# Moving two thirds of the ada sums of a 256-token network into its first feed-forward part, with two-part fp32r row sums

## The chip, the cores and the metric

The kernel runs on one core of a Trainium2 chip. The metric is the device time of one execution in microseconds. TensorE does the matrix products, VectorE and ScalarE the elementwise work, POOL (GpSimd) issues some transfers and does a few elementwise steps, SP (SyncE) issues the transfers of the weights. Each engine runs its own instructions in order and waits on semaphores.

## The reference

One sequence of 256 tokens of width 1024 passes a first block of two layers and a second block of one layer. Everything is fp32. What matters here:

```
# first block, layer 0: even mixer; layer 1: odd mixer (two attentions)
x = layer_norm(ALPHA * x + mixer(x), ln_mix_g[l], ln_mix_b[l])
x = layer_norm(ALPHA * x + (silu(x @ w_gate[l]) * (x @ w_up[l])) @ w_down[l], ln_ffn_g[l], ln_ffn_b[l])

# second block
mod = split(silu(c) @ ada_w + ada_b, 6)                  # six rows of 1024
a = rmsnorm(x, g_pre) * (1 + mod[1]) + mod[0]
x = x + mod[2] * rmsnorm(short_gated_conv(a), g_post)
f = (relu(modulate(rmsnorm(x, g_pre_ff), mod[3], mod[4]) @ mlp_w_in) ** 2) @ mlp_w_out
x = x + mod[5] * rmsnorm(f, g_post_ff)
```

`silu(c) @ ada_w` is a vector of 1024 times a matrix of 1024 x 6144 (24 MB).

## The kernel before, in words

The program is one sequence of stages: even mixer, first feed-forward part (`ffn0`), odd mixer, second feed-forward part (`ffn1`), short conv (`sc`), MLP. Weights come in chunks of 1 MB. SP loads a chunk (`raw`) as soon as a slot of its ring of four or six is free. ScalarE copies it to fp32r (`hi`), VectorE subtracts (`lo = raw - hi`); this is a *split*. TensorE then does three fp32r products for one fp32 product (hi·hi, hi·lo, lo·hi). `split(upto)` stands at written-out places in the programs of ScalarE and VectorE, so the order is that of the code: no scheduler is involved, and an instruction that waits holds back all behind it on its engine.

A feed-forward part has 11 blocks (`NF`), one per 256 columns of the hidden layer. In block `i` TensorE does the gate chunk and the up chunk (`col`, 48 matmuls of 256 columns each) into PSUM banks 6 and 7 or 4 and 5 in turn; ScalarE does silu, VectorE the product `hid`, ScalarE `hid_hi`, VectorE `hid_lo`. Up to block 8 TensorE then does the down chunk of the block before (`rows_full`, 24 matmuls of 512 columns). Blocks 9 and 10 have none; after block 10 the last three down chunks are done for token half 0 and then for half 1, the third one closing each half (`rows_end`). The layer norm's sum (`ln_sum`, L1645) reads that.

The ada product is done beside `ffn1`: POOL loads 24 pieces of ada_w, 1 MB each, in turn into the buffers `sq` and `r`; VectorE multiplies each by a column of silu(c) and adds it into `modrow` (`ada_step`, L423), two or three per block. `mod_sums(m)` (L699) sums row m over the 128 partitions with a matmul against ones, into the PSUM banks that the block before has just left, and `mod_copy` (L1217) on ScalarE brings the sum, now on all partitions, back to `modrow`. The table `MOD_AT = {4: 0, 5: 1, 7: 2, 8: 3, 10: 4}` says after which block which row is summed; the sixth is in `sc`. TensorE does not write the banks again before the copy. At the end of `ffn1` VectorE does `gained` (L1723) for rows 1 and 2: it multiplies them by two gain rows, which POOL loads into `sq` after the last ada product (`gain_row`, L482). Behind `gained` VectorE has the split of the last down chunk, two more splits and then `ln_sum`.

POOL also loads the two rows (gain and bias) of each layer norm into `lnrow` (`ln_rows`, L478), those of the next norm as soon as the one before is through.

`modrow` lies in memory that the even and the odd mixer use for other things; it is free only in the feed-forward parts and behind them.

Of the kernel before, what the change touches and what calls it, by code (L numbers as in the profile page):

```python
# [6 lines left out]
F32 = mybir.dt.float32  # L7
# [62 lines left out]
def build(nc, A, out):  # L70
    ctx = ExitStack()
    with ctx:
# [24 lines left out]
        ones = sb("ones", [P, P])  # L97
        d_skip = sb("d_skip_sb", [P, KT])
# [99 lines left out]
        def bank2(b):  # L198
            return PS[:, b, :].rearrange("p (a s) -> p a s", a=2)

# [212 lines left out]
        ADA_BLOCKS = range(1, 10)  # L413
        MOD_AT = {4: 0, 5: 1, 7: 2, 8: 3, 10: 4}
        MOD_LAST = 5
# [57 lines left out]
        def _(pool):  # L473
# [46 lines left out]

            pool.wait_ge(*sig_at("ln0", "x", 4))
            ln_rows("ln1")
            pool.wait_ge(*sig_at("ln1", "x", 4))
# [5 lines left out]
            pool.tensor_tensor(kr_cos[rr, :], kr[rr, 0, :], cos, ALU.mult).then_inc(sem("kr_cos"), 1)  # L529
            pool.wait_ge(*norm("kvn", "var", 1))  # L530
            for q in range(4):
# [3 lines left out]
                    .then_inc(sem("qm_cos"), 1)  # L535
# [3 lines left out]
                             .to_broadcast([32, MLA_H, S])).then_inc(sem("kr_rot"), 1)  # L539

            pool.wait_ge(*sig_at("ln2", "x", 4))
            ln_rows("ln3")
            pool.memset(modrow[:, :, :], 0.0).then_inc(sem("ada_zero"), 1)
            pool.wait_ge(sem("ada_zero"), 1)
            pool.dma_start(modrow[0:1, :, :].rearrange("p m d -> p (m d)"), A["ada_b_2"][0:1, :])\
                .then_inc(sem("ada_bias"), 16)
            for n in range(ADA_N):
                if n >= 2:
                    pool.wait_ge(sem("ada_fma"), n - 1)
                pool.dma_start(ada_raw[n % 2], A["ada_w_2"][0][n % KT * P:(n % KT + 1) * P, n // KT * CH:(n // KT + 1) * CH])\  # L550
                    .then_inc(sem(f"ada_landed{n % 2}"), 16)
# [8 lines left out]
        def _(pe):  # L560
# [134 lines left out]
            def mod_sums(m, bank):  # L695

                pe.wait_ge(sem("ada_fma"), KT * (m // 2 + 1))
                for n in range(2):
                    last = pe.matmul(PS[:, bank + n, :], ones[:, :], modrow[:, m, n * HB:(n + 1) * HB], start=True, stop=True)  # L699
                last.then_inc(sem("mod_sum"), 1)  # L700

            def ffn(name, operand, after, src):
# [13 lines left out]
                for i in range(1, NF):  # L716
                    b = 6 - 2 * (i % 2)
                    pe.wait_ge(hid_done, o + i)
                    if name == "ffn1" and i - 1 in MOD_AT:
                        pe.wait_ge(sem("mod_row"), MOD_AT[i - 1] + 1)  # L720
# [5 lines left out]
                    if name == "ffn1" and i in MOD_AT:  # L726
                        pe.wait_ge(hid_done, o + i + 1)
                        mod_sums(MOD_AT[i], 6 - 2 * ((i - 1) % 2))
# [164 lines left out]
            base = first["odd"]  # L893
            for h in range(2):
# [83 lines left out]
            def scores(a):  # L978
# [5 lines left out]
                if a == FOX_H:  # L984
                    pe.wait_ge(sem("odd_evac"), 19)
                    pe.wait_ge(sem("kr_rot"), 1)
# [54 lines left out]
            ffn("ffn1", "ln2", "pre", r_tok)  # L1041

# [20 lines left out]
            for q in range(1, 4):  # L1063
                for part in range(3):
                    col(at["sc", "c", q] + part, sc_bank(3 * q + part), x_hi, x_lo)
                    if q == 1 and part == 0:
# [4 lines left out]
                        mod_sums(MOD_LAST, 0)  # L1071
                if q == 1:
                    pe.wait_ge(sem("mod_row"), MOD_LAST + 1)
# [45 lines left out]
        def _(act):  # L1119
# [19 lines left out]
            def preload(func):  # L1139

                act.wait_ge(sem("eps_set"), 1)
# [71 lines left out]

            def mod_copy(m, bank):
# [5 lines left out]
            def ffn(name):  # L1220
# [11 lines left out]
                for i in range(1, NF):  # L1232
                    g = at[name, "g", i]
                    split(g + 2)
                    act.wait_ge(chunk_used, g + 1)
# [8 lines left out]
                    if name == "ffn1" and i in MOD_AT:  # L1244
                        mod_copy(MOD_AT[i], 6 - 2 * ((i - 1) % 2))
# [17 lines left out]
            act.activation(head_vec[:, 2:3], head_vec[:, 1:2], ACT.Exp).then_inc(sem("a_ready"), 1)  # L1263
# [8 lines left out]
            act.activation(silu_c[:, :], vecs[:, 2, 0:8], ACT.Silu).then_inc(sem("silu_c_ready"), 1)  # L1272
# [868 lines left out]
```

## Time and profile before

| | us |
|---|---|
| median of 3 runs | 980.95 |
| lowest, highest | 979.12, 981.13 |
| profiled execution | 980.15 |
| its span, first to last instruction | 978.27 |
| TensorE matmul busy in the span | 944.3 (97%) |
| VectorE busy | 645.9 (66%) |
| ScalarE busy | 466.6 (48%) |
| mean granted TensorE clock | 0.997 |

Times inside the span count from its first instruction. "Busy" of TensorE counts matmuls that overlap one another; the distance from one start to the next is what a matmul costs in a row of them. `idle before` in a timeline names what ended the idle time of the engine. A row of a timeline may merge several instructions (xN). `ffn0` lies at about 150 to 330 us, `ffn1` at about 495 to 690, `sc` at 690 to 790.

### The profile page before, as it was taken

What the parts mean: (1) busy time and instruction counts of PE and PEld (TensorE: products, weight loads), DVE (VectorE), ACT (ScalarE), POOL (GpSimd) and SP (SyncE); (2) the same over time, 40 slices, a digit from 0 to 9 for tenths busy, and PEclk for the clock granted to TensorE, in tenths of its full rate; (3) what the DMA queues carried; (4) which work ended last, traced back from release to release, by engine and by line L of the source; (5) the groups of instructions that cost most, each with busy time, mean ns of one, the idle gap of its engine ahead of it and who ended that gap; (6) DMA issues with size and microseconds to landing.
All of it is one profiled execution on the core that took longest, in us unless ns stands there. A gap on an engine that the chain in (4) does not pass through costs nothing.

```text
span 978.3 us, 15123 instructions
## 1 busy us (share of the span) xinstructions
PE 944.3 (97%) x6537; PEld 862.8 (88%) x6537; DVE 645.9 (66%) x737; ACT 466.6 (48%) x577; POOL 62.0 (6%) x79
## 2 busy tenths in 40 slices
PE   6999989999999999999899999999899999999997
PEld 6999879999999799876699989998799989999986
DVE  4976896645454863676659788788866865555554
ACT  6556744434343465755544343445344644444442
POOL 2034000000000000220030001000000000000000
PEclk9999999999999999999999999999999999999999
DMA  9744466565565453412579999995566456566531
GB/s 280 239 131 130 136 205 219 186 195 178 181 203 177 130 173 110 133 44 87 176 283 331 381 317 338 308 348 165 185 198 198 130 175 213 175 194 191 174 128 44
DMA packets 122282, 190.52 MB, mean 195 GB/s; under 512 B 6566, under 2 KB 103080, under 8 KB 119144
## 3 DMA queue, kind: packets, MB, share of 16 engines
q1 hardware_dynamic: 115184, 156.94, 49.5%
q0 software_dynamic: 5616, 31.78, 8.8%
q8 instruction: 52, 0.85, 0.3%
q10 hardware_dynamic: 1416, 0.83, 0.3%
q14 instruction: 14, 0.11, 0.0%
HBM read 188.49 MB, written 1.05 MB: 194 GB/s over the span
## 4 chain that ended last, share of the span: by engine, by line
PE 80%; DVE 10%; ACT 5%; issue 3%; DMA 1%; DVEq 0%; POOL 0%; ACTq 0%
PE PS L565 15%; PE PS L567 15%; PE PS L566 15%; PE PS L572 10%; PE PS L574 9%; PE PS L573 9%; DVE lo L1575 3%; ACT hi L1136 2%; PE PS L699 1%; PE PS L663 1%; DMA raw<-even_w_in 1%; DVE r L1645 1%; ACT hid L1437 1%; DMA sq<-norm_gains 1%; ACT sq L1321 1%
## 5 line engine op out<-in xcount | busy, mean ns | idle before, releaser
L1575 DVE TENSOR_TENSOR lo<-raw,hi 128x2048 fp32r<-128x2048 f32 (+2 forms) x150 | 336.1, 2258 | 168.8 <-ACT hi L1136 168.6
L565 PE MATMUL PS<-x_hi,hi 128*128 128x256 f32 x1320 | 374.4, 284 | 1.9 <-DVE x_lo L1772 1.9
L567 PE MATMUL PS<-x_hi,lo 128*128 128x256 f32 x1320 | 372.3, 282 | 0.0
L566 PE MATMUL PS<-x_lo,hi 128*128 128x256 f32 x1320 | 371.7, 282 | 0.0
L1136 ACT ACTIVATE hi<-raw 128x2048 fp32r<-128x2048 f32 (+2 forms) x150 | 278.1, 1880 | 10.2 <-DMA raw<-even_w_in 8.0
L565 PEld LDWEIGHTS PS<-x_hi,hi 128*128 128x128 f32 x1320 | 251.2, 190 | 4.3 <-DVE lo L1575 2.3
L566 PEld LDWEIGHTS PS<-x_lo,hi 128*128 128x128 f32 x1320 | 251.2, 190 | 1.9 <-issue 0.5
L567 PEld LDWEIGHTS PS<-x_hi,lo 128*128 128x128 f32 x1320 | 251.2, 190 | 0.0
L572 PE MATMUL PS<-hi,hid_hi 128*128 128x512 f32 x352 | 141.2, 401 | 1.1 <-DVE lo L1575 0.7
L574 PE MATMUL PS<-hi,hid_lo 128*128 128x512 f32 x352 | 138.6, 394 | 0.0
L573 PE MATMUL PS<-lo,hid_hi 128*128 128x512 f32 x352 | 138.5, 393 | 0.0
L572 PE MATMUL PS<-hi,x_hi 128*128 128x256 f32 (+1 forms) x256 | 81.7, 319 | 7.7 <-DVE x_lo L1674 3.5
L572 PEld LDWEIGHTS PS<-hi,hid_hi 128*128 128x128 f32 x352 | 66.1, 188 | 17.5 <-issue 3.7
L574 PEld LDWEIGHTS PS<-hi,hid_lo 128*128 128x128 f32 x352 | 66.0, 188 | 15.6
L574 PE MATMUL PS<-hi,x_lo 128*128 128x256 f32 (+1 forms) x256 | 79.8, 312 | 0.0
L573 PE MATMUL PS<-lo,x_hi 128*128 128x256 f32 (+1 forms) x256 | 79.6, 311 | 0.0
L573 PEld LDWEIGHTS PS<-lo,hid_hi 128*128 128x128 f32 x352 | 66.0, 188 | 15.1 <-issue 1.2
L1238 ACT ACTIVATE gate_s<-PS 128x512 f32<-128x512 f32 x20 | 12.0, 599 | 103.2 <-PE PS L567 103.2
L572 PEld LDWEIGHTS PS<-hi,x_hi 128*128 128x128 f32 x256 | 48.8, 191 | 13.3 <-issue 8.1
L574 PEld LDWEIGHTS PS<-hi,x_lo 128*128 128x128 f32 x256 | 48.8, 191 | 2.8
L1243 ACT ACTIVATE hid_hi<-hid 128x512 fp32r<-128x512 f32 x20 | 12.6, 632 | 80.9 <-DVE hid L1750 80.9
L573 PEld LDWEIGHTS PS<-lo,x_hi 128*128 128x128 f32 x256 | 49.0, 191 | 2.5
(280 smaller groups left out, 825.5 us busy)
## 6 DMA issues: line engine op xcount, KB each, us to landing
raw<-ffn_w_gate SPq DMA_DIRECT2D x22, 1024.0 KB, 5.4
raw<-ffn_w_up SPq DMA_DIRECT2D x22, 1024.0 KB, 5.5
raw<-ffn_w_down SPq DMA_DIRECT2D x22, 1024.0 KB, 5.0
raw<-mlp_w_in SPq DMA_DIRECT2D x16, 1024.0 KB, 5.6
raw<-mlp_w_out SPq DMA_DIRECT2D x16, 1024.0 KB, 5.0
sq<-ada_w POOLq DMA_DIRECT2D x12, 1024.0 KB, 6.3
r<-ada_w POOLq DMA_DIRECT2D x12, 1024.0 KB, 7.2
raw<-sc_w_in SPq DMA_DIRECT2D x12, 1024.0 KB, 5.3
```

The source lines that it names most:

```text
L565: pe.matmul(dst, wh, hi, start=start, stop=False, skip_group_check=True)
L566: pe.matmul(dst, wh, lo, start=False, stop=False, skip_group_check=True)
L567: return pe.matmul(dst, wl, hi, start=False, stop=stop_, skip_group_check=True)
L572: pe.matmul(dst, hi, wh, start=start, stop=False, skip_group_check=True)
L573: pe.matmul(dst, hi, wl, start=False, stop=False, skip_group_check=True)
L574: return pe.matmul(dst, lo, wh, start=False, stop=stop_, skip_group_check=True)
L663: last = pe.transpose(PS[:, 2 * h + n, j * P:(j + 1) * P], src[:, h, o:o + P], ident)
L699: last = pe.matmul(PS[:, bank + n, :], ones[:, :], modrow[:, m, n * HB:(n + 1) * HB], start=True, stop=True)
L1136: act.activation(split_view("hi", c), split_view("raw", c), ACT.Copy).then_inc(hi_split, 1)
L1238: act.activation(gate_s[:, i % 2, :, :], bank2(6 - 2 * (i % 2)), ACT.Silu).then_inc(silu, 1)
L1243: act.activation(hid_hi[:, i % 3, :, :], hid[:, i % 2, :, :], ACT.Copy).then_inc(hi_done, 1)
L1575: dve.tensor_tensor(split_view("lo", c), split_view("raw", c), split_view("hi", c).bitcast(F32), ALU.subtract)\
```

## The change

- The 24 ada products are divided: 16 (rows 0 to 3) run beside `ffn0`, two in each of blocks 1 to 8, and 8 (rows 4 and 5) beside `ffn1`, one in each of blocks 1 to 8. POOL clears `modrow` and loads the bias row in two parts.
- `MOD_AT` now has a table for each part: in `ffn0` rows 0 to 3 after blocks 6, 7, 9, 10; in `ffn1` rows 4 and 5 after blocks 9 and 10. The sum in `sc` is gone.
- Before a sum, ScalarE rounds the row to fp32r (`mod_high`) and VectorE takes the remainder (`mod_low`) into `mod_part`; `mod_sums` is four fp32r matmuls against `ones_r`.
- `mod_part` shares its memory with `lnrow`. So `ln_rows("ln1")` waits for the fourth sum and `ln_rows("ln3")` for the sixth, where each used to be issued before the part began.
- Rows 0 to 3 are written to a DRAM tensor `mods` after `ffn0` and read back, onto all partitions, at the start of `ffn1`. VectorE and ScalarE wait for the write before they use that memory in the odd stage.
- Some semaphores are merged (`cleared`, `rope_cos`, `a_silu_c`), with the same order of what is waited for.

```diff
-        lnrow = sb("lnrow", [P, 2, D])
+        with ExitStack() as row_views:
+            lnrow = sb("lnrow", [P, 2, D], F32, row_views)
+        mod_part = sb("mod_part", [P, 2, D], F32R)
...
+        mods = nc.dram_tensor("mods", (1, 4 * D), F32, kind="Internal").ap()
...
-        ADA_BLOCKS = range(1, 10)
-        MOD_AT = {4: 0, 5: 1, 7: 2, 8: 3, 10: 4}
-        MOD_LAST = 5
+        ADA_STEPS = {"ffn0": (0, 2 * KT), "ffn1": (2 * KT, ADA_N)}
+        MOD_AT = {"ffn0": {6: 0, 7: 1, 9: 2, 10: 3}, "ffn1": {9: 4, 10: 5}}
...
+            def ada_loads(m0, m1):
+                pool.memset(modrow[:, m0:m1, :], 0.0).then_inc(sem("ada_zero"), 1)
+                pool.wait_ge(sem("ada_zero"), 1 + (m0 > 0))
+                pool.dma_start(modrow[0:1, m0:m1, :].rearrange("p m d -> p (m d)"), A["ada_b_2"][0:1, m0 * D:m1 * D])\
+                    .then_inc(sem("ada_bias"), 16)
+                if m0:
+                    pool.wait_ge(sem("mods_moved"), 16)
+                    pool.dma_start(modrow[:, 0:4, :].rearrange("p m d -> p (m d)"), mods[0:1, :].to_broadcast([P, 4 * D]))\
+                        .then_inc(sem("mods_moved"), 16)
+                for n in range(m0 * KT // 2, m1 * KT // 2):
...
             pool.wait_ge(*sig_at("ln0", "x", 4))
+            ada_loads(0, 4)
+            pool.wait_ge(sem("mod_sum"), 4)
             ln_rows("ln1")
+            pool.wait_ge(sem("mod_row"), 4)
+            pool.dma_start(mods[0:1, :], modrow[0:1, 0:4, :].rearrange("p m d -> p (m d)")).then_inc(sem("mods_moved"), 16)
             pool.wait_ge(*sig_at("ln1", "x", 4))
             ln_rows("ln2")
...
             pool.wait_ge(*sig_at("ln2", "x", 4))
+            ada_loads(4, 6)
+            pool.wait_ge(sem("mod_sum"), 6)
             ln_rows("ln3")
...
             def mod_sums(m, bank):
-                pe.wait_ge(sem("ada_fma"), KT * (m // 2 + 1))
+                pe.wait_ge(sem("mod_low"), m + 1)
                 for n in range(2):
-                    last = pe.matmul(PS[:, bank + n, :], ones[:, :], modrow[:, m, n * HB:(n + 1) * HB], start=True, stop=True)
+                    for part in range(2):
+                        last = pe.matmul(PS[:, bank + n, :], ones_r[:, :], mod_part[:, part, n * HB:(n + 1) * HB],
+                                         start=part == 0, stop=part == 1, skip_group_check=True)
...
+            def mod_high(m):
+                act.wait_ge(sem("ada_fma"), KT * (m // 2 + 1))
+                if m:
+                    act.wait_ge(sem("mod_sum"), m)
+                act.activation(mod_part[:, 0, :], modrow[:, m, :], ACT.Copy).then_inc(sem("mod_high"), 1)
...
+            def mod_low(m):
+                dve.wait_ge(sem("mod_high"), m + 1)
+                dve.tensor_tensor(mod_part[:, 1, :], modrow[:, m, :], mod_part[:, 0, :].bitcast(F32), ALU.subtract)\
+                   .then_inc(sem("mod_low"), 1)
...
+            dve.wait_ge(sem("mods_moved"), 16)
             dve.memset(neg_both[:, :].bitcast(F32), 0.0)
```

POOL's program at the end of `ffn1`, before the change (`sq<-norm_gains` are the gain rows that `gained` needs, `lnrow<-norm_gains` two later ones):

```order
L550 DMA sq<-ada_w 128x2048 [waits ada_fma]
L550 DMA r<-ada_w 128x2048 [waits ada_fma]
L482 DMA sq<-norm_gains 128x1024 [waits ada_fma]
L482 DMA sq<-norm_gains 128x1024
L482 DMA lnrow<-norm_gains 128x1024 [waits ln_x]
```

And after it:

```order
L538 DMA sq<-ada_w 128x2048 [waits ada_fma]
L538 DMA r<-ada_w 128x2048 [waits ada_fma]
L482 DMA lnrow<-ln_ffn_g 128x1024 [waits mod_sum]
L482 DMA lnrow<-ln_ffn_b 128x1024
L486 DMA sq<-norm_gains 128x1024 [waits ada_fma]
L486 DMA sq<-norm_gains 128x1024
L486 DMA lnrow<-norm_gains 128x1024 [waits ln_x]
```

ln3's two rows have moved from the head of `ffn1` to a place ahead of the gain rows, behind a wait for the sixth sum.

VectorE's program at the same end, after the change (L1788 is `hid`, L1754 `gained`, L1603 a split, L1673 `ln_sum`); apart from the line `mod_part` its order there is that of before:

```order
L1760 TENSOR_TENSOR mod_part<-modrow,mod_part 128x1024 [waits mod_high]
L1603 TENSOR_TENSOR lo<-raw,hi 128x2048 [waits hi_split]
L1788 TENSOR_TENSOR hid<-gate_s,PS 128x512 [waits chunk_used,ffn_silu]
L1793 TENSOR_TENSOR hid_lo<-hid,hid_hi 128x512 [waits ffn_hid_hi]
L1754 SCALAR_TENSOR_TENSOR modrow<-modrow,sq 128x1024 [waits gain_landed,mods_moved] x2
L1603 TENSOR_TENSOR lo<-raw,hi 128x2048 [waits hi_split] x3
L1673 SCALAR_TENSOR_TENSOR r<-x_tok,PS 128x512 [waits ffn1_acc,gained]
```

TensorE's program from block 9 to block 10 of `ffn0`, before:

```order
L565 MATMUL PS<-x_hi,hi 128x256
L566 MATMUL PS<-x_lo,hi 128x256
L567 MATMUL PS<-x_hi,lo 128x256
L565 MATMUL PS<-x_hi,hi 128x256 [waits lo_split,ffn_hid]
L566 MATMUL PS<-x_lo,hi 128x256
```

And after:

```order
L582 MATMUL PS<-x_hi,hi 128x256
L583 MATMUL PS<-x_lo,hi 128x256
L584 MATMUL PS<-x_hi,lo 128x256
L717 MATMUL PS<-mod_part,ones_r 128x512 [waits mod_low,ffn_hid]
L717 MATMUL PS<-mod_part,ones_r 128x512 x3
L582 MATMUL PS<-x_hi,hi 128x256 [waits lo_split,mod_row,ffn_hid]
L583 MATMUL PS<-x_lo,hi 128x256
```

A sum stands directly between the two blocks, and the next block's first matmul waits for `mod_row`, ScalarE's copy of it.

## Rows read from the trace of the kernel before

**Rows 1.** The page, busy time and share of the span by engine.
```profile
PE 944.3 (97%) x6537; PEld 862.8 (88%) x6537; DVE 645.9 (66%) x737; ACT 466.6 (48%) x577; POOL 62.0 (6%) x79
```

**Rows 2.** Chain of waits: start us, us, what.
```profile
665.65 5.46 DMA sq<-norm_gains
...
717.84 1.72 PE PS L699 x4
```

**Rows 3.** Timeline of TensorE, last block of `ffn1`: start us, us, instruction.
```profile
668.07 1.88 PE L699 MATMUL PS<-modrow,ones 128*128 128x512 f32 x4
...
670.02 0.40 PE L573 MATMUL PS<-lo,hid_hi 128*128 128x512 f32 x1
670.25 0.39 PE L574 MATMUL PS<-hi,hid_lo 128*128 128x512 f32 x1
```

**Rows 4.** Timeline of VectorE, end of `ffn1`.
```profile
668.34 0.69 DVE L1750 TENSOR_TENSOR hid<-gate_s,PS 128x512 f32<-128x512 f32 x1 [1.10 <-PE PS L567]
...
671.21 2.36 DVE L1723 SCALAR_TENSOR_TENSOR modrow<-modrow,sq 128x1024 f32<-128x1024 f32 x2 [0.79 <-DMA sq<-norm_gains]
673.49 6.69 DVE L1575 TENSOR_TENSOR lo<-raw,hi 128x2048 fp32r<-128x2048 f32 x3
680.09 1.28 DVE L1645 SCALAR_TENSOR_TENSOR r<-x_tok,PS 128x512 f32<-128x512 f32 x2
...
688.71 1.28 DVE L1645 SCALAR_TENSOR_TENSOR r<-x_tok,PS 128x512 f32<-128x512 f32 x2
```

**Rows 5.** Timeline of TensorE, the three last down chunks of `ffn1`.
```profile
675.91 0.47 PE L572 MATMUL PS<-hi,hid_hi 128*128 128x512 f32 x1 [0.37 <-DVE lo L1575]
...
686.89 0.39 PE L574 MATMUL PS<-hi,hid_lo 128*128 128x512 f32 x1
```

**Rows 6.** Timeline of ScalarE, end of `ffn1`.
```profile
669.06 0.63 ACT L1243 ACTIVATE hid_hi<-hid 128x512 fp32r<-128x512 f32 x1 [4.15 <-DVE hid L1750]
669.98 1.03 ACT L1217 ACTIVATE modrow<-PS 128x1024 f32<-128x1024 f32 x1 [0.29 <-PE PS L699]
```

**Rows 7.** Timeline of ScalarE in `ffn0`: first ordinary block, last block.
```profile
167.22 0.59 ACT L1238 ACTIVATE gate_s<-PS 128x512 f32<-128x512 f32 x1
...
312.19 0.60 ACT L1238 ACTIVATE gate_s<-PS 128x512 f32<-128x512 f32 x1 [2.53 <-PE PS L567]
...
318.74 0.63 ACT L1243 ACTIVATE hid_hi<-hid 128x512 fp32r<-128x512 f32 x1 [4.15 <-DVE hid L1750]
319.28 5.51 ACT L1136 ACTIVATE hi<-raw 128x2048 fp32r<-128x2048 f32 x3
```

**Rows 8.** Timeline of ScalarE in `ffn1`: first ordinary block, last block.
```profile
510.48 0.59 ACT L1238 ACTIVATE gate_s<-PS 128x512 f32<-128x512 f32 x1
...
662.51 0.60 ACT L1238 ACTIVATE gate_s<-PS 128x512 f32<-128x512 f32 x1 [2.53 <-PE PS L567]
```

**Rows 9.** Timeline of POOL: clearing of modrow, first ada load, gain rows.
```profile
495.57 5.24 POOL L543 MEMSET modrow<- 128x6144 f32 x1
...
501.60 0.56 POOL L550 DMA_DIRECT2D sq<-ada_w  x1
...
665.13 1.05 POOL L482 DMA_DIRECT2D sq<-norm_gains  x2 [12.58 <-DVE modrow L423]
```

**Rows 10.** Timeline of VectorE, end of `ffn0`: first use of ln1's row.
```profile
330.58 1.41 DVE L1658 SCALAR_TENSOR_TENSOR r<-r,moments,lnrow 128x512 f32<-128x512 f32 x2
```

**Rows 11.** DMA issues from 480 to 520 us: count, size, us to landing.
```profile
r<-ada_w POOLq DMA_DIRECT2D x1, 1024.0 KB, 10.0
lnrow<-ln_ffn_g POOLq DMA_DIRECT2D x1, 512.0 KB, 4.0
lnrow<-ln_ffn_b POOLq DMA_DIRECT2D x1, 512.0 KB, 4.9
```

**Rows 12.** Busy by stretch; last: granted clock, DMA share, GB/s.
```profile
666.00:673.00 7.00, 7.00 (x37) 5.45 (x36) 4.42 (x5) 3.65 (x4) 0.18 (x1) 1.00 1.03 344
```

**Rows 13.** The same for a stretch before `ffn0`; first column TensorE busy (matmuls).
```profile
133.50:136.90 3.40, 3.40 (x10) 2.63 (x9) 3.30 (x4) 0.00 (x0) 0.00 (x0) 0.50 0.00 0
```

More of the change, by code:

```diff
@@ L725, in ffn @@
                     col(at[name, "g", i] + 1, b + 1, x_hi, x_lo)
-                    if name == "ffn1" and i in MOD_AT:
+                    if i in MOD_AT[name]:
                         pe.wait_ge(hid_done, o + i + 1)
-                        mod_sums(MOD_AT[i], 6 - 2 * ((i - 1) % 2))
+                        mod_sums(MOD_AT[name][i], 6 - 2 * ((i - 1) % 2))
                     if i <= NF - TAIL:
@@ L1234, in ffn @@
                     split(g + 2)
+                    if i in MOD_AT[name]:
+                        mod_high(MOD_AT[name][i])
                     act.wait_ge(chunk_used, g + 1)
@@ L1261, in _ @@
             act.wait_ge(sem("heads_landed"), 16 * 3)
-            act.activation(head_vec[:, 2:3], head_vec[:, 1:2], ACT.Exp).then_inc(sem("a_ready"), 1)
+            act.activation(head_vec[:, 2:3], head_vec[:, 1:2], ACT.Exp).then_inc(sem("a_silu_c"), 1)
             split(3)
@@ L1271, in _ @@
             act.wait_ge(sem("vecs_ready"), 1)
-            act.activation(silu_c[:, :], vecs[:, 2, 0:8], ACT.Silu).then_inc(sem("silu_c_ready"), 1)
+            act.activation(silu_c[:, :], vecs[:, 2, 0:8], ACT.Silu).then_inc(sem("a_silu_c"), 1)
             base = first["even"]
@@ L1719, in gained @@
             def gained(m, i, plus):
-                dve.wait_ge(sem("mod_row"), m + 1)
+                if m < 4:
+                    dve.wait_ge(sem("mods_moved"), 32)
+                else:
+                    dve.wait_ge(sem("mod_row"), m + 1)
                 dve.wait_ge(sem("gain_landed"), 32 * (i // 2 + 1))
@@ L1731, in ffn @@
                     g = at[name, "g", i]
-                    ada = list(range(ADA_N * (i - 1) // 9, ADA_N * i // 9)) if name == "ffn1" and i in ADA_BLOCKS else []
-                    if ada and i == 1:
-                        dve.wait_ge(sem("silu_c_ready"), 1)
-                        dve.wait_ge(sem("ada_bias"), 16)
+                    n0, n1 = ADA_STEPS[name]
+                    ada = list(range(n0 + (n1 - n0) * (i - 1) // 8, n0 + (n1 - n0) * i // 8)) if 1 <= i <= 8 else []
+                    if i == 1:
+                        dve.wait_ge(sem("a_silu_c"), 2)
+                        dve.wait_ge(sem("ada_bias"), 16 + 16 * (name == "ffn1"))
                     split(g + 2)
-                    if len(ada) > 2:
-                        ada_step(dve, ada.pop(0))
                     if i == 0:
@@ L1746, in ffn @@
                     else:
+                        if i in MOD_AT[name]:
+                            mod_low(MOD_AT[name][i])
                         split(g + 3)
```

63 lines of the change are left out of this document (30 added, 33 removed).

## The prediction, made before the result was known

> **What bounds the kernel now.** I read the page's busy times first: TensorE is busy for 97% of the span and VectorE for 66% [rows 1]. So a matmul removed in the middle of a stage counts in full, and VectorE or a DMA counts only where TensorE waits for it. The chain of waits says where that is: one such place is the end of the second feed-forward part. There the chain leaves TensorE and runs over the transfer of two gain rows, 5.46 us, and later passes the fp32 row sum in the short-conv stage, 1.72 us [rows 2]. The timelines of each engine at that end (about 668 us) then give the order and the spare time.
>
> I call T the start of the row sum in the last block, 668.07 us [rows 3]. From there: VectorE starts `hid` at T+0.27, scales the two modulation rows by the gains (`gained`) at T+3.14, splits three weight chunks from T+5.42 and starts the layer norm's sum at T+12.02 [rows 4]. The first of the three chunks is the last one that TensorE needs: it resumes at 675.91 (T+7.84), after a last wait of 0.37 us [rows 5]. So the end is VectorE's, and whatever delays `gained` delays both. The profiled run took 980.15 us, of which the span is 978.27; it lies 0.8 below the median of the runs, 980.95. The sum is made against 980.15.
>
> **The change, part by part.**
>
> *The sums.* Before, one `mod_sums` is two fp32 matmuls, in the profile four records 0.43 us apart, 1.72 us. After, it is four fp32r matmuls of 128x512. Such matmuls start 0.23 us apart [rows 3], so 0.93 us.
> - Second part: four sums at blocks 4, 5, 7, 8 go, 4 x 1.72 = -6.88. The fifth sits after T, in time that VectorE covers.
> - Short-conv stage: the sixth goes, -1.72 [rows 2]. The next chunk's split is then ready only about 0.1 us after TensorE could use it, so I take -1.6.
> - First part: rows 0 and 1 at blocks 6 and 7 are followed by 5.6 us of down-projection, which hides the copy back: 2 x 0.93 = +1.86.
> - Rows 2 (first part) and 4 (second part) are put in block 9. After block 9 no down-projection comes, and the next block's first matmul writes the very PSUM banks of the sum, behind a wait for ScalarE's copy out of them. That copy stands behind `hid_hi`. In the last block `hid_hi` starts at T+0.99 and lasts 0.63, and the copy lasts 1.03 [rows 6]. The same order at block 9 ends the copy 0.99+0.63+1.03 = 2.65 us after the block's matmuls, in place of 0. So 2 x 2.65 = +5.30, of which 3.4 is TensorE standing still. Before, no sum stood in block 9.
> - Row 3, first part's last block: the copy now stands between `hid_hi` (318.74) and the three splits behind it (319.28) [rows 7]. VectorE waits for those splits, so +0.95 (1.03 less the overlap of neighbouring instructions).
>
> Subtotal: -6.88 - 1.6 + 1.86 + 5.30 + 0.95 = -0.37 us. The cheaper sums are eaten by where they stand.
>
> *The 16 products moved, with 16 MB of loads.* The second part already carried 24 in nine blocks: its first ordinary block's gate to its last took 662.51-510.48 = 152.03 us, less 6.88 of sums 145.15, against 312.19-167.22 = 144.97 in the first part without any [rows 7, 8]. So this load costs 0.2 us at most, and taking it off gives 0.2 at most: 0. `mod_high` and `mod_low`, one pass over 128x1024 each on ScalarE and VectorE (1.03 us for the copy of that size [rows 6]), lie in the same idle time. The clearing of modrow took 5.24 us for 6144 columns [rows 9], so 3.5 for 4096; with the bias it ends about 160, before the second block needs it: 0.
>
> *Rows through DRAM.* The write goes out after the first part's last copy, and the waits for it (VectorE before its memsets, ScalarE before v_tok; behind them all the odd stage's splits) come behind the layer norm that ends the part; that of the second part starts its sum at T+12.02 [rows 4]. Even the slowest landing below, 10 us, is hidden: 0, bounded by 0 and 0.5. The read back is 2 MB ahead of the ada loads; the ln3 rows that stood there (1 MB) are gone and the clearing is 3.5 us shorter, so the first product still finds its data: 0, up to +2.
>
> *ln1's rows* are now requested after the fourth sum, about T+1.4. In the first part's clock their use is at 330.58 [rows 10], 12.8 us after its T (318.74 less the 0.99 above, 317.75). They need 4.9 us alone [rows 11], 10 with competition: hidden.
>
> *ln3's rows and the gain rows.* This is the largest term. POOL is in order. Before, it issued the two gain rows at 665.13 [rows 9], T-2.94, straight after the last product. After, it first waits for the sixth sum, which ends T+0.93 plus 0.2, then issues ln3's two rows, then the two gain rows. With POOL's reaction of 0.3 the first issue is T+1.41 and the first gain row T+2.47: 5.41 us later than before. Behind `gained` on VectorE stand the last down chunk's split, which TensorE waits for, two more splits and the layer norm's sum.
> Lower bound of the shift S of `gained`: 5.41, if the landing takes what it took. Upper: 2 MB of rows share the engines with the 1 MB weight chunk that SP issues around T. The engines moved 344 GB/s while the gain rows and that chunk ran [rows 12]; a rate of 300 to 330 for 3.15 MB beginning at T+2 gives T+11.5 to T+12.5, and with landing and start T+13.4: S = 10.3. The nearest row: two 1 MB ada loads beside SP's chunks, the first issued at 501.60 and the second half a microsecond later [rows 9], of which the second landed 10.0 us after its issue, so 10.6 after the first [rows 11]. The same 2 MB in the same company: T+1.41+10.6 = T+12.0. I take S = 8.7, between that and the rate. TensorE then stands still for some 9 us.
>
> On this the Trainium skill has two sayings in "DMA: Bandwidth & Descriptors". "Issuing engines are not separate DMA queues": POOL's rows and SP's chunk run on the same 16 engines and interleave; the trace agrees, with its 10.0 against 4.9 us, and that speaks against the change. "Anatomy of one DMA — SWDGE (gpsimd) path" fits 2.0 us plus bytes over 436 GB/s: for the four rows together an estimate of 6.8 us, thus S of about 5; the sum would be 985 instead of 988.5.
>
> **Sum:** 980.15 - 0.37 + 8.7 = 988.5 us.
>
> **The rivals.**
> 1. *Quick rows.* The four rows overlap so well that the gain rows land as they did: S = 5.4. For it: one pair lands in 4.0 and 4.9 us [rows 11]. Against it: that was 1 MB alone. 980.15-0.37+5.4 = 985.2.
> 2. *The clock falls.* After sparse matmuls the granted clock was 0.50 from 133.5 to 136.9, 10 matmuls in 3.4 us where 14.6 fit [rows 13]. The new stop of 9 us at the second part's end could do the same. TensorE's last tail matmul starts at 686.89 [rows 5], 1.8 us before VectorE's second half (688.71) [rows 4], so 1.5 us lost is hidden; with the low clock for twice as long, 1.1 shows: 989.6. The Trainium skill ("TensorE: Matmul & The Clock Gate", "HAM oscillation — how this bites in real kernels") says that long DMA waits put the gate back to half speed; in this trace only that one stretch inside the work shows it.
> 3. *Crowding at the second part's start.* The 2 MB read back takes 6.1 us at 344 GB/s [rows 12] and pushes chunks or the first product out by that; if their lead covers half of it, +2 to +3: 991. Against it: the 1 MB of ln3's rows that stood there before is gone.
> 4. *Faster: the gain rows land before VectorE asks.* `gained` would start at T+2.3 behind `hid_lo`, S = -0.8: 979.0. It decides at S = 0.37, where the rows cost what the sums give. Against it: they would have to land in 2.1 us after the first issue, and the fastest landing is 4.0 [rows 11]. Relief of VectorE in the second part would be the only other gain, and that is 0.2 at most.
> 5. *The change does less than it says*, that is, the rows were never waited for at either end and all else cancels: 980. For it only that the subtotal is near zero.
>
> **How the numbers follow.** Forecast 0.60, quick rows 0.17, clock 0.05, crowding 0.09, faster 0.05, nothing 0.04. A measurement of this kernel can tell about 0.2% (2 us) from no change. The forecast and rivals 1 to 3 are slower by more than that: 0.91; faster 0.05; within 0.04. The forecast's own range, S from 7 to 10.3, is 986.8 to 990.1. The range asked for reaches down to the quick rows less half a microsecond and up to crowding: 984.5 to 991.5.
>
> **What would show it.** The sums' four matmuls 0.23 us apart. A gap of about 1.7 us on TensorE ahead of the last gate chunk in both parts, released by ScalarE's modrow copy. At the end of the second part: POOL issuing four rows after the last sum, VectorE idle 8 to 9 us before L1754 (`gained`), released by DMA sq<-norm_gains, and TensorE idle about 9 us before the last down chunk. In the first part no idle time before L1686 released by a lnrow transfer. No wait of POOL, ACT or VectorE named by mods longer than 0.5 us. The prediction is wrong if the two parts' VectorE load turns out to hold up TensorE, if `gained` starts within 6 us of T, or if block 9 shows no gap.

## The result and the profile after

The changed kernel takes 992.73 us, the median of 4 runs (991.3 to 993.05), against 980.95 for the kernel before: ratio 1.0118, 95% interval 1.0104 to 1.0133. I had forecast 988.5 and a range up to 991.5. The direction was right, the size 4.2 us short, and the time lies outside the range. Beside the experiments the kernel before was run again, 15, 17 and 23 times; the medians are 981.28, 981.35 and 981.36 (979.25 to 983.4 in all).

The profiled run of the changed kernel took 992.73 us, so the two traces differ by 12.58. TensorE's busy time has not grown, only its share [rows 1]:

```profile
PE 944.8 (95%) x6537; PEld 866.6 (87%) x6537; DVE 652.2 (66%) x744; ACT 471.7 (48%) x583; POOL 62.3 (6%) x83
```

**The end of the second feed-forward part.** The chain of waits, start, length and what, answers to the first row of [rows 2]. Where 5.46 us of transfer stood, there are now 9.97, and ahead of them POOL's issues, released by the sum (L717):

```profile
671.02 0.95 PE PS L717 x4
671.97 0.28 issue
672.25 1.05 POOL lnrow L482 x2
673.30 0.51 POOL sq L486
673.81 9.97 DMA sq<-norm_gains
```

T, the start of the sum in the last block, is 670.86 here. VectorE's timeline in the same place, against [rows 4]:

```profile
671.13 0.69 DVE L1788 TENSOR_TENSOR hid<-gate_s,PS 128x512 f32<-128x512 f32 x1 [1.11 <-PE PS L584]
...
683.88 2.36 DVE L1754 SCALAR_TENSOR_TENSOR modrow<-modrow,sq 128x1024 f32<-128x1024 f32 x2 [10.67 <-DMA sq<-norm_gains]
686.15 6.69 DVE L1603 TENSOR_TENSOR lo<-raw,hi 128x2048 fp32r<-128x2048 f32 x3
```

`gained` (L1754) starts at T+13.02 in place of T+3.14: a shift of 9.88 us, where I had 8.7. TensorE stands still for 11 us, and when it resumes its matmuls take longer than the 0.39 us of [rows 5]:

```profile
688.59 0.77 PE L589 MATMUL PS<-hi,hid_hi 128*128 128x512 f32 x1 [11.06 <-DVE lo L1603]
689.15 0.63 PE L590 MATMUL PS<-lo,hid_hi 128*128 128x512 f32 x1
689.58 0.63 PE L591 MATMUL PS<-hi,hid_lo 128*128 128x512 f32 x1
```

The stretches show why; the columns are stretch, length, busy time of PE, PEld, VectorE, ScalarE and POOL, then the granted clock, DMA share and GB/s:

```profile
676.00:688.00 12.00, 1.53 (x7) 0.92 (x5) 4.12 (x3) 4.27 (x4) 0.00 (x0) 0.71 0.47 162
688.00:694.00 6.00, 5.42 (x13) 4.29 (x14) 5.44 (x4) 0.00 (x0) 0.00 (x0) 0.50 0.01 3
694.00:696.00 2.00, 2.00 (x9) 1.58 (x8) 1.88 (x4) 0.00 (x0) 0.00 (x0) 0.82 0.00 0
```

The granted clock fell during the stop, at 681.0, and stayed at 0.50, the lower of the two levels, for the first 6.1 us of the tail (688.59 to 694.7): a matmul every 0.43 us in place of 0.23. That is the second rival, and it came on top of the forecast. Part of what it cost can be seen on VectorE. In the kernel before, the two instructions of the layer norm's sum follow each other with no wait [rows 4]; here the second one waits 0.64 us for TensorE's last matmul of the half:

```profile
692.76 0.68 DVE L1673 SCALAR_TENSOR_TENSOR r<-x_tok,PS 128x512 f32<-128x512 f32 x1
694.08 0.69 DVE L1673 SCALAR_TENSOR_TENSOR r<-x_tok,PS 128x512 f32<-128x512 f32 x1 [0.64 <-PE PS L591]
```

**Block 9.** TensorE's timeline: the sum, and then the next gate chunk's first matmul.

```profile
656.64 1.09 PE L717 MATMUL PS<-mod_part,ones_r 128*128 128x512 f32 x4
659.27 0.36 PE L582 MATMUL PS<-x_hi,hi 128*128 128x256 f32 x1 [1.53 <-issue]
```

From the sum's start it is 2.63 us, where I had 2.65; the gap itself is 1.53 us, where I had 1.7. The wait is put down to "issue"; ScalarE's timeline shows what ended it, the copy out of the banks behind `hid_hi`, in the order of [rows 6]:

```profile
657.63 0.63 ACT L1271 ACTIVATE hid_hi<-hid 128x512 fp32r<-128x512 f32 x1 [4.04 <-DVE hid L1788]
658.16 1.00 ACT L1243 ACTIVATE modrow<-PS 128x1024 f32<-128x1024 f32 x1
```

**The whole, stage by stage.** I compared the start of each block's `gate_s` in both traces. The difference grows by 1.50 up to the first part (153.28 to 154.78), then by 0.92, 0.92, 2.71 and, by the start of the second part, 0.92. In the second part it falls by four times 1.71 or 1.72 and grows by 2.70 at block 9. From that part's last block to short-conv it grows by 11.18, and in short-conv it falls by 1.36. Sum: 12.6.

The first 1.50 arise where both kernels have the same code, 1.3 of them between 12 and 18 us. In the trace before, TensorE does 10 matmuls a microsecond from 12 us on; in the other it does 6 or 7 until 15 us. The first line is of the trace before, the second of the trace after:

```profile
12.00:13.00 1.00, 1.00 (x10) 1.00 (x10) 1.00 (x3) 1.00 (x3) 0.00 (x0) 1.00 1.10 370
12.00:13.00 1.00, 1.00 (x7) 1.00 (x6) 1.00 (x3) 1.00 (x3) 0.00 (x0) 1.00 1.09 369
```

The 1.00 of the granted clock is no reading here: its record begins at 10.6 us in the trace before and only at 15.4 in the other. Fewer matmuls up to just that moment fit a lower clock before it; no experiment tested this.

### The profile page after: what moved, and what is told of

Its sections match the earlier page's. It is cut to its first block, busy times and chain, and to the rows that moved or that the text cites. A ratio compares the mean times of both kernels' runs of the same rounds, so it can differ in the third digit from the quotient of the medians.

```text
span 990.8 us, 15148 instructions
## 1 busy us (share of the span) xinstructions
PE 944.8 (95%) x6537; PEld 866.6 (87%) x6537; DVE 652.2 (66%) x744; ACT 471.7 (48%) x583; POOL 62.3 (6%) x83
## 4 chain that ended last, share of the span: by engine, by line
PE 82%; DVE 8%; ACT 5%; issue 3%; DMA 2%; POOL 0%; DVEq 0%; ACTq 0%
PE PS L582 16%; PE PS L584 16%; PE PS L583 16%; PE PS L589 10%; PE PS L590 10%; PE PS L591 10%; DVE lo L1603 2%; ACT hi L1155 2%; DMA sq<-norm_gains 1%; PE PS L680 1%; DMA raw<-even_w_in 1%; ACT hid L1465 1%; ACT sq L1349 1%; DVE gate_s L2024 1%; PE PS L1040 0%
## 5 line engine op out<-in xcount | busy, mean ns | idle before, releaser
L1603 DVE TENSOR_TENSOR lo<-raw,hi 128x2048 fp32r<-128x2048 f32 (+2 forms) x150 | 336.1, 2258 | 169.9 <-ACT hi L1155 169.7
L590 PEld LDWEIGHTS PS<-lo,hid_hi 128*128 128x128 f32 x352 | 66.7, 190 | 14.3
```

The source lines that it names most:

```text
L590: pe.matmul(dst, hi, wl, start=False, stop=False, skip_group_check=True)
L1603: dve.tensor_tensor(split_view("lo", c), split_view("raw", c), split_view("hi", c).bitcast(F32), ALU.subtract)\
```

## The experiments

Runs differ by up to 3.3 us before the first feed-forward part begins: its first `gate_s` starts at 152.90 to 156.15 us in the thirteen profiles, in no relation to the edits. Six profiles start by 153.68, and in them the record at 1.00 begins at 9.7 to 10.6 us; seven start at 154.68 or later, and in them it begins, or comes back from 0.50, only at 15.2 to 17.5 us. So the table gives, beside the medians, the profiled run's time less that start, which is free of it. It is not free of low clock later on: in the profiles of gain_early and filler a stretch at 0.50 inside the odd stage (422.7 to 426.1, 425.2 to 428.6) adds 1.0 us that the others do not have. Each ratio is the recorded one, against the runs of the kernel before of the same round (for `after` the 4 of the first); it is not the quotient of the two medians.

```
kernel            median   ratio to before (95%)      profiled less start
before            981.36   (last 23 runs)              826.87
after             992.73   1.0118 (1.0104, 1.0133)    837.95
gain_early        980.60   0.9995 (0.9985, 1.0006)    826.87
gain_first_late   988.59   1.0077 (1.0058, 1.0096)    833.24
off_nine          987.65   1.0070 (1.0055, 1.0086)    834.06
filler            994.84   1.0145 (1.0126, 1.0164)    841.73
filler95          992.41   1.0108 (1.0090, 1.0126)    837.74
chunk_later       990.40   1.0090 (1.0073, 1.0106)    835.25
fp32_sums         983.66   1.0018 (1.0008, 1.0028)    829.02
both              977.30   0.9957 (0.9942, 0.9972)    822.38
gained_last       982.99   1.0018 (1.0008, 1.0029)    828.30
late_copy         976.38   0.9964 (0.9950, 0.9978)    821.40
all_second        980.75   0.9997 (0.9983, 1.0011)    827.72
```

**gain_early: the gain rows at their old place**

```
             ada_loads(4, 6)
+            pool.wait_ge(sem("ada_fma"), ADA_N)
+            gain_row(0)
+            gain_row(1)
             pool.wait_ge(sem("mod_sum"), 6)
             ln_rows("ln3")
-            pool.wait_ge(sem("ada_fma"), ADA_N)
-            gain_row(0)
-            gain_row(1)
```

> The changed kernel, with POOL's two gain rows issued right behind the last ada product, ahead of its wait for the sixth sum; ln3's two rows stay behind that wait. Account A (the 11.2 us lost at the end of the second feed-forward part are VectorE's wait for the gain rows, 9.9 us, and 1.3 us of low clock after TensorE's stop): gained starts near T+3.1 again, no low clock at that end, 992.7 - 11.2 = 981.5 us. Rival B (ln3's rows, still late, are needed by the layer norm and take the gain rows' place): VectorE idle before L1686 for 3 us or more, 984.5 or above. Rival C (the wait is for the traffic as a whole, not for the order on POOL): gained still 5 us late, 987.

980.60 us: the two moved lines take back 12 us. VectorE's timeline at that end:

```profile
671.67 0.69 DVE L1793 TENSOR_TENSOR hid_lo<-hid,hid_hi 128x512 fp32r<-128x512 f32 x1 [0.70 <-ACT hid_hi L1271]
672.28 2.35 DVE L1754 SCALAR_TENSOR_TENSOR modrow<-modrow,sq 128x1024 f32<-128x1024 f32 x2
```

`gained` follows `hid_lo` with no wait, at T+2.27 (T is 670.01): 0.87 earlier than in the kernel before, where it waited 0.79 for the rows. The stage is 0.9 us shorter than in the kernel before, where in the changed kernel it was 11.2 longer. ln3's rows, still issued after the sum, are nowhere waited for, which ends rival B; rival C falls too. The clock is 1.00 through the tail; it goes to 0.50 from 692.3 to 695.7, at the start of short-conv, where no lost time is seen.

**gain_first_late: the gain rows ahead of ln3's, both late**

```
             pool.wait_ge(sem("mod_sum"), 6)
-            ln_rows("ln3")
             pool.wait_ge(sem("ada_fma"), ADA_N)
             gain_row(0)
             gain_row(1)
+            ln_rows("ln3")
```

> The changed kernel, with the wait for the sixth sum kept ahead of all four rows, but the two gain rows issued before ln3's two. Splits the late issue from the traffic ahead. If the rows stand in line on one queue and move at 268 GB/s behind SP's chunk (as in the trace of the changed kernel), the gain rows land near T+8.7, shift of gained 5.6 instead of 9.9, 992.7 - 4.3 = 988.4 us, or 987.1 if TensorE's clock then holds. If the queue order doesn't matter (all four share): no change, 992.5. If one pair lands in 4.9 us whatever SP does: shift 3.3, 986 or 985.

988.59 us. The order on the queue counts: `gained` starts at T+9.69, a shift of 6.55, one us more than expected. POOL's queue still stands in line; no pair of rows came in 4.9 us. TensorE's first tail matmul was at 683.53, and the clock:

```profile
676.00:684.00 8.00, 0.47 (x1) 0.50 (x2) 5.17 (x4) 2.56 (x3) 0.00 (x0) 0.72 0.50 203
684.00:686.00 2.00, 2.00 (x6) 1.52 (x6) 2.00 (x2) 0.00 (x0) 0.00 (x0) 0.50 0.00 0
686.00:688.00 2.00, 2.00 (x10) 1.60 (x9) 2.00 (x2) 0.00 (x0) 0.00 (x0) 0.89 0.03 8
```

The clock fell here too, but was back 2.9 us after the first tail matmul. The stage takes 6.53 us longer than before, the shift and nothing more, and VectorE does not wait for TensorE in the layer norm's sum:

```profile
687.71 1.28 DVE L1673 SCALAR_TENSOR_TENSOR r<-x_tok,PS 128x512 f32<-128x512 f32 x2
```

**off_nine: rows 2 and 4 summed at block 8**

```
-        MOD_AT = {"ffn0": {6: 0, 7: 1, 9: 2, 10: 3}, "ffn1": {9: 4, 10: 5}}
+        MOD_AT = {"ffn0": {6: 0, 7: 1, 8: 2, 10: 3}, "ffn1": {8: 4, 10: 5}}
...
-  n0 + (n1 - n0) * (i - 1) // 8, n0 + (n1 - n0) * i // 8)) if 1 <= i <= 8
+  n0 + (n1 - n0) * (i - 1) // 7, n0 + (n1 - n0) * i // 7)) if 1 <= i <= 7
```

> The changed kernel, with rows 2 and 4 summed at block 8 in place of block 9 and the products spread over seven blocks instead of eight (up to three in a block). Account A (at block 9 TensorE stands still for the copy, 2.71 us a place; at block 8 a down-projection covers it, 0.92): 992.7 - 2 x 1.79 = 989.1 us. Rival: the three products in a block, or the scaling to two parts, hold up VectorE and through it TensorE at block 8: 991 to 993.

987.65 us, and 3.9 less than the changed kernel by the profiles, for 3.6 expected. In the first part 0.92 comes at block 8 and 2.71 goes at block 9; in the second 0.87 comes and 2.77 goes. That block 9 costs a stop and block 8 none is shown; three products in a block hold nothing up here.

**filler and filler95: TensorE kept at work during the stop**

Matmuls of constants into a bank that is free there; their result isn't used.

```
+                        if name == "ffn1" and not h:
+                            for n in range(150):      # filler95: 95
+                                pe.matmul(PS[:, 6, 0:P], ones_r[:, :], ones_r[:, :], start=True, stop=True)
                         rows_end(*down(i), h, name)
```

> The changed kernel, with 150 matmuls of 128x128 of constants on TensorE ahead of the last down chunk of the second feed-forward part, where it stands idle for 11 us; their result is not used. Account A (1.3 us of the loss are the low clock, 0.50 until 694.3, after the stop): the granted clock stays 1.00 to the end of the tail and the time falls by about 1.3 to 991.4 us. Rival (those 1.3 us are hidden behind VectorE's layer norm, or are something else): 992.7, with the clock at 1.00.

> As the filler before, with 95 matmuls of 128x128 in place of 150: in the profile of that run one took 0.111 us, so 95 take 10.5 us and end before the 11.2 us of waiting do. Account A (low clock costs 1.3 us): granted clock 1.00 through the tail, the end of the second feed-forward part loses 9.9 us in place of 11.2, 992.7 - 1.3 = 991.4 us. Rival (the slow tail is hidden behind VectorE): 992.7.

The first was a miss of mine: one such matmul takes 0.111 us, so 150 ran until 695.7 and held up the tail itself, 994.84 us. It shows one thing: with no gap the granted clock stayed at 1.00 through the stop and the tail.

```profile
680.00:690.00 10.00, 10.00 (x92) 10.00 (x91) 2.80 (x3) 1.90 (x3) 0.00 (x0) 1.00 0.39 153
688.00:694.00 6.00, 6.00 (x56) 6.00 (x56) 6.00 (x5) 0.00 (x0) 0.00 (x0) 1.00 0.00 0
```

With 95 the matmuls ended at 688.49, and as the rows landed a microsecond later in that run (`gained` at T+14.04, shift 10.90), TensorE stood idle for 1.41 us. Of the filler95 profile:

```profile
688.00:690.00 2.00, 0.59 (x6) 0.45 (x5) 2.00 (x2) 0.00 (x0) 0.00 (x0) 0.84 0.00 0
690.00:692.00 2.00, 2.00 (x5) 1.61 (x6) 2.00 (x2) 0.00 (x0) 0.00 (x0) 0.50 0.00 0
692.00:694.00 2.00, 2.00 (x8) 1.60 (x8) 2.00 (x2) 0.00 (x0) 0.00 (x0) 0.80 0.00 0
```

The clock fell after all, but came back 2.9 us into the tail, and the stage took 10.89 us longer for a shift of 10.90: nothing on top. The median of 992.41 tells no difference from 992.73, since the later landing ate the gain. So the expectation failed as to the clock and the time; what holds is a comparison over the profiles. Where the low clock lasts 2.9 us of the tail (gain_first_late, filler95) the stage loses the shift and no more, and VectorE does not wait for TensorE there; where it lasts 6.1, 5.9 and 5.5 us (the changed kernel, off_nine, chunk_later) the stage loses 1.3, 1.2 and 1.0 us more than the shift, and in all three VectorE has the wait of 0.64 us. No run took the low clock away and left the late rows as they were, so the 1.3 us rest on this comparison.

**chunk_later: SP's weight chunk held back**

```
+                if c == first["sc"] + 2:
+                    sp.wait_ge(sem("gain_landed"), 32)
```

In the changed kernel POOL issued the rows from 672.25 on. The queues of the DMA engines (queue, packets, MB, share), first from 671 to 675, then from 676 to 684:

```profile
q1 hardware_dynamic: 858, 0.88, 71.0%
...
q0 software_dynamic: 540, 1.95, 70.7%
```

Until 675 only SP's chunk moves (q1), though POOL had issued all four rows by 674.3; from 676 on only POOL's rows, 1.95 MB in some 8 us. In the microsecond between, both move:

```profile
q1 hardware_dynamic: 182, 0.17, 50.0%
q0 software_dynamic: 36, 0.15, 40.4%
```

Their first packet starts at 675.21, 2.96 us after the first issue.

> The changed kernel, with SP's third short-conv chunk (1 MB, issued at T+0.2) held until the two gain rows have landed. In the trace of the changed kernel the four rows, issued from T+1.4, start to move only at T+4.5, when that chunk is through. Account A (the rows stand behind the chunk on the same engines): they start to move near T+2.9, the gain rows land 1.6 to 3.1 us sooner, shift of gained 6.8 to 8.3 in place of 9.9, about 990.4 us. Rival (the rows' late start is POOL's own queue, its descriptors): gained at T+13 as before, 992.7, or later if the chunk is now missed: 994.

990.40 us. `gained` starts at T+10.43, a shift of 7.29 in place of 9.88: 2.6 of the shift are due to the chunk. The rows' first packet now starts 1.24 us after their first issue, 1.7 sooner; the other 0.9 us come between the first packet and the landing of the last row. The profiles without this edit that have the same order of issues put `gained` at T+12.99 to T+14.72, so the gain is outside their spread, though it is read from one profile. The rows' own 2 MB, at 258 GB/s from 674 to 682, are the rest:

```profile
q0 software_dynamic: 567, 2.06, 80.3%
```

**fp32_sums: the move alone**

The sums are two fp32 matmuls again, `mod_high` and `mod_low` are gone, and the rows of ln1 and ln3 and the gain rows are issued at their old places.

```
-                pe.wait_ge(sem("mod_low"), m + 1)
+                pe.wait_ge(sem("ada_fma"), KT * (m // 2 + 1))
...
+                    last = pe.matmul(PS[:, bank + n, :], ones[:, :], modrow[:, m, n * HB:(n + 1) * HB], start=True, stop=True)
...
+            ln_rows("ln3")
             ada_loads(4, 6)
-            pool.wait_ge(sem("mod_sum"), 6)
-            ln_rows("ln3")
```

> The changed kernel without the two-part fp32r sums: each is again two fp32 matmuls of the whole row, in the same blocks (6, 7, 9, 10 and 9, 10), and as nothing then shares memory with the layer norm's rows, those and the gain rows are issued where they were before the change. So only the move is left. Account A: no stop at the end of the second part; blocks 6 and 7 1.72 us each, blocks 9 about 3.0 each (sum and copy), the first part's end 1.4 to 1.9, four sums fewer in the second part (-6.88) and none in short-conv (-1.4): 981 + 2.8 = 983.8 us. Rival (the stop at the end has to do with the move, not with the rows' place in POOL's order): 990 or more.

983.66 us, as forecast from the terms. Blocks 6 and 7 cost 1.70 each and block 9 of the second part 3.09; the stage's end loses nothing (-0.42). The 11 us stop comes with the two-part sums and the order of issues on POOL that was written for their shared memory, and not with the move; gain_early showed that the memory can be shared without it. What the move alone costs is 2.2 us by the profiles (829.02 against 826.87).

**both, and late_copy**

`both` is gain_early and off_nine together. `late_copy` also lets ScalarE copy the last block's sum out behind its chunk splits:

```
-                    if i in MOD_AT[name]:
+                    if i in MOD_AT[name] and i < NF - 1:
                         mod_copy(MOD_AT[name][i], 6 - 2 * ((i - 1) % 2))
                     if i < NF - 1:
                         split(g + 4)
+                split(first["odd" if name == "ffn0" else "sc"] + 1)
+                mod_copy(3 if name == "ffn0" else 5, 4)
```

> The changed kernel with the gain rows issued right behind the last product and rows 2 and 4 summed at block 8: the two mends that the first runs measured apart. If they add: 980.6 - 3.6 = 977.0 us, faster than the kernel before by 0.4%. Rival (they overlap, since VectorE's end of the part sets the time once its wait is gone, or block 8's load delays it): 979 to 980.6.

> The kernel with both mends (977.3 us), and in the last block of each part ScalarE copies the row sum out only behind its three chunk splits in place of ahead of them. Account A (the row of the first part's last block costs 0.9 us because the copy delays the splits that VectorE and then TensorE wait for): -0.9, 976.4 us; in the second part nothing, since VectorE is busy there with the gains. Rival (the 0.9 us are the sum's own four matmuls): 977.3.

977.30 us: the two mends add, and this beats the kernel before (ratio 0.9957). 976.38 us with the late copy: from block 10 to the start of the second part the difference to before changes by -0.03 in place of the +0.86 of `both`, so row 3's cost was the copy's place and not the sum. The runs alone could not tell 0.9 us: the two ratios, 0.9957 and 0.9964, lie within each other's interval. ScalarE's timeline in late_copy at the end of the first part, against [rows 7]:

```profile
321.89 0.63 ACT L1271 ACTIVATE hid_hi<-hid 128x512 fp32r<-128x512 f32 x1 [4.15 <-DVE hid L1790]
322.43 3.70 ACT L1155 ACTIVATE hi<-raw 128x2048 fp32r<-128x2048 f32 x2
```

**gained_last: asking for the late rows later**

```
-                    if name == "ffn1" and i == NF - 1:
-                        gained(1, 0, 1.0)
-                        gained(2, 1, 0.0)
...
             ln_sum("ln3", "ffn1", 0, 0)
             ln_rest("ln3", 0)
+            gained(1, 0, 1.0)
+            gained(2, 1, 0.0)
```

> The changed kernel with POOL's order as it is (ln3's rows and gain rows issued late, landing near T+13), but VectorE scales by the gains only behind the layer norm's first half, just ahead of the first use of the result, and no longer ahead of the three chunk splits. Account A (TensorE stops only because the split of its last chunk is queued on VectorE behind the instruction that waits for the rows): the splits and the layer norm run from T+2.3, the gain rows have landed by the time they are asked for, no stop, 992.7 - 11.2 - 0.9 (before, gained itself waited 0.8) = 980.6 to 981.5 us. Rival (the late rows cost their time wherever they are asked for, ln3's own rows first): 985 or more.

982.99 us. POOL's order is that of the changed kernel, the rows are no sooner (the last one lands at T+14.3, in the changed kernel at T+12.9), and yet some 10 us come back: what stopped TensorE was the splits queued behind the waiting instruction. VectorE's timeline:

```profile
673.33 6.70 DVE L1603 TENSOR_TENSOR lo<-raw,hi 128x2048 fp32r<-128x2048 f32 x3 [2.02 <-ACT hi L1155]
...
685.55 2.35 DVE L1754 SCALAR_TENSOR_TENSOR modrow<-modrow,sq 128x1024 f32<-128x1024 f32 x2
```

`gained` waits for nothing. The median is 1.5 to 2.4 us above what I expected. VectorE now idles 2.02 us ahead of the splits, since ScalarE's copy and split come first, and `gained` then stands on the way from the layer norm to the next operand. TensorE stands idle for 3.0 us up to 690.15, and the clock is low again, from 689.7 to 696.5:

```profile
691.00:694.00 3.00, 2.35 (x12) 1.98 (x11) 2.84 (x5) 1.19 (x2) 0.00 (x0) 0.50 0.37 117
```

**all_second: without the move**

All 24 products and six sums in the second part, sums at blocks 4, 5, 7, 8, 9 and 10, no copy through DRAM, gain rows early; the main lines:

```
-        ADA_STEPS = {"ffn0": (0, 2 * KT), "ffn1": (2 * KT, ADA_N)}
-        MOD_AT = {"ffn0": {6: 0, 7: 1, 9: 2, 10: 3}, "ffn1": {9: 4, 10: 5}}
+        ADA_STEPS = {"ffn0": (0, 0), "ffn1": (0, ADA_N)}
+        MOD_AT = {"ffn0": {}, "ffn1": {4: 0, 5: 1, 7: 2, 8: 3, 9: 4, 10: 5}}
```

> What the move itself is worth: all 24 products and all six sums in the second feed-forward part, nothing kept in DRAM, with the two-part sums and the gain rows issued behind the last product; sums at blocks 4, 5, 7, 8, 9 and 10, three products a block. Against the kernel before: in the second part four sums at 0.92 and one at block 9 with the copy (2.7) in place of four at 1.72: -0.5; the end -0.4 to -0.9; short-conv -1.36: 981 - 2.5 = 978.5 us. Rival (three products, a scaling and a split in a block are too much for VectorE, and the move was needed for the cheap sums): over 981.

980.75 us, 2.2 above what I expected. In the profile the sums at blocks 5 and 7 save 0.79 each, but blocks 8 and 9 together cost 4.2, where 1.9 would follow from the terms (0.92 in place of 1.72, and 2.70). The last product runs at 648.70, and behind it on VectorE stand a chunk split, the scaling to parts and another split. So `hid` of block 9 starts only at 656.68, `hid_hi` and the copy come behind it, and the next gate chunk starts 3.51 us after the sum, in place of 2.63.

```profile
648.70 2.35 DVE L427 SCALAR_TENSOR_TENSOR modrow<-r,silu_c,modrow 128x2048 f32<-128x2048 f32 x1 [1.97 <-DMA r<-ada_w]
650.97 2.29 DVE L1593 TENSOR_TENSOR lo<-raw,hi 128x2048 fp32r<-128x2048 f32 x1
653.17 1.22 DVE L1747 TENSOR_TENSOR mod_part<-modrow,mod_part 128x1024 fp32r<-128x1024 f32 x1
```

With all six sums in one part, then, the load on VectorE did count in this run. That is 0.9 of the excess. The larger part is something else: behind that wait the granted clock was 0.50 from 660.3 to 663.7, and from that gate chunk's start to the last block's sum it took 13.07 us, in place of 11.59 in the changed kernel. And the profiled run, at 982.40, is one of the slow ones of a wide spread, 977.13 to 982.79 in twelve runs. The kernel to compare with is gain_early, which has the same two-part sums, the same early gain rows and also a sum at block 9, but with the move: 980.60 against 980.75. So these runs show no gain from the move. `both` is 3.5 us faster than all_second, but it also has its sums off block 9; six sums in the second part with none at block 9 were not tried.

## Why the prediction came out short

The mechanism of the largest term was right: the gain rows come late, VectorE waits for them and TensorE for VectorE. Three steps failed. The shift S was put at 8.7 and measured 9.88. The low clock behind the stop was left out of the sum as a rival with a chance of 0.05, and cost about 1.3. And the base was one profile that begins early, 1.5 us against the profile after.

*The sums.* The subtotal of -0.37 held: +0.92, +0.92, +2.71, +0.92, four times -1.71 or -1.72, +2.70 and -1.36 make -0.05. The largest part of the difference is short-conv, -1.36 for my -1.6. off_nine and late_copy showed the mechanisms at block 9 and at the first part's end one by one.

*Products, rows through DRAM, ln1's rows.* Cost nothing, as forecast: the block to block distances in between agree within 0.02 us, and the whole odd stage adds nothing.

*The shift S of `gained`.* The mechanism was right and the term too small: 9.88 for 8.7 (+1.2 us). The first issue came at T+1.39, as worked out (T+1.41). What failed is the landing: I took two ada loads as the nearest row, 10.6 us after the first issue, and it was 11.6. Those loads made up the same volume, but here the rows did not move until SP's chunk was nearly through, and then at 244 GB/s on average, less than the 300 and more that I had used. My upper bound of 10.3 had held it, but it is no bound: in filler95 and filler, with the same order of issues, S was 10.90 and 11.58. chunk_later measured the chunk's share, 2.6 us.

*The clock.* Here a step of the reasoning failed, not a size. I made "the clock falls" a rival with a chance of 0.05, though its condition, a stop of 9 us, was the forecast itself. It had to be added to the sum: it cost 1.3 us, and I had priced it at 1.1. I had held against it that one stretch alone of the trace before shows it [rows 13]; but in that trace TensorE has no idle gap of even 2.5 us, so it held no row on what follows a stop of 9. The Trainium skill ("TensorE: Matmul & The Clock Gate", "HAM oscillation — how this bites in real kernels") says that waiting for DMAs puts the gate back to half speed. This case agrees: 0.50 behind the stop, 1.00 throughout where filler matmuls left no gap.

*The start.* 1.5 us of the difference between the two traces arise before the first part, and are no effect of the change: the fastest start of all is one of the edited kernels with the same code there (152.90), the slowest another (156.15). I had taken a profile of 980.15 as the base; the median over the last 23 runs is 1.2 us higher. The 1.3 us that arise between 12 and 18 us go with how soon the clock's record at 1.00 begins, as shown above.

Together: 1.2 + 1.3 + 1.5 + 0.3 for the sums are 4.3, and 4.2 us were missed.

*The rivals.* Quick rows: no, the landing came late and not early. Crowding at the second part's start: no, 0.0. Faster: its mechanism is real, gain_early shows just this start of `gained` right behind `hid_lo`, but only once the rows are issued early. "Nothing": no.

*The range.* With the upper bound of S (+1.6) and the clock (+1.1) it would have reached 991.2 from the forecast alone, and the run-to-run spread of some 2 us, known from the first three runs, was not in it. It should have gone to 993, by what was known then; with the S of the two filler runs, higher still.

## What to carry to other kernels

When memory is shared between an early and a late use, look at everything that is queued behind the new wait on the issuing engine: here two lines that needed no such wait stood behind it and cost 12 us, and issuing them first gave all of it back. An instruction that waits for a transfer belongs behind the work that others wait for: moved so on VectorE, it gave 10 us back with the rows as late as ever. And a rival whose condition is your own forecast is no rival but a term: a long stop of TensorE is priced with the slow matmuls behind it, here 0 to 1.3 us, by how much of them VectorE covers.

The version that came of it (both parts of the change, gain rows issued first, rows 2 and 4 at block 8, the last copy behind the splits) runs in 976.38 us, with a recorded ratio of 0.9964 (0.9950 to 0.9978) to the kernel before. What it owes to the cheaper sums, the early gain rows and the blocks chosen is shown; that it needs the move is not.

## What the hardware showed that I had not expected

POOL's four row transfers, issued at 672.25 to 674.3, hardly shared the engines with the 1 MB chunk that SP had issued a microsecond earlier (671.05): until 675 only the chunk moved, from 675 to 676 both, and then only the rows. About 1.2 us of that delay is there without the chunk too (chunk_later). The Trainium skill ("DMA: Bandwidth & Descriptors", "Issuing engines are not separate DMA queues") says that the transfers of all engines run on the same 16 and interleave; the first half agrees, the second was seen here only in the chunk's last microsecond. Elsewhere it holds: in the trace before, packets of both queues moved in every microsecond from 506 to 511.

The rows, broadcast to 128 partitions, moved at 244 GB/s from 676 to 684 and at 258 GB/s from 674 to 682 in chunk_later, while SP's chunk just before came near 390. These are averages over an uneven flow: from one microsecond to the next the changed kernel's rows went from 12 to 422 GB/s. The landing varied too: in the five profiles with this order of issues `gained` started between T+12.99 and T+14.72 where it waited for the rows, and in gained_last, where it did not, the last row landed at T+14.3.

It is not only the long stops that bring the lower clock level about. A gap of 1.41 us on TensorE, after 10.7 us of small matmuls, was followed by 2.9 us of matmuls at 0.50 (filler95). And in the odd stage of gain_early the clock was 0.50 from 422.7 to 426.1 with no idle gap over 1.3 us in the 25 us before, while the kernel before, with the same gaps in the same places, kept 1.00.
